# A two-layer decoder trunk on one core: first attention reordered, the expert loop's hidden values in two halves, slot sums made once, heads alternating in stick-breaking

## The reference

```
for i in range(2):
    h = rms_norm(x, attn_norm[i])
    x = x + (swa_sink_attention if i == 0 else stick_breaking_attention)(h, ...)
    h = rms_norm(x, ffn_norm[i])
    x = x + (swiglu if i == 0 else moe_swiglu)(h, ...)
out = rms_norm(x, final_norm)
# swa: q, k, v = split(h @ w_qkv + b_qkv); 16 query heads, 2 key/value heads of 64; window of 128
#      s = q k' / 8 + bias[bucket(distance)]; p = softmax over keys and one learned sink; (p v) @ w_o
# stick-breaking: z = q k' / 8, s < t only; log_fail = log_sigmoid(-z)
#      a = exp(log_sigmoid(z) + reverse cumsum of log_fail, without itself); (a v) @ w_o; 16 heads of 64
# swiglu: (silu(h Wg) * (h Wu)) Wd, width 2816
# moe: each token takes the top 2 of 8 experts by a router; an expert is a swiglu of width 3584
```

## Time and profile before

| | |
|---|---|
| median of 3 runs (lowest, highest) | 1461.12 us (1460.49, 1463.1) |
| the profiled execution, its span | 1462.36 us, 1460.6 us |
| PE busy | 1417.1 us (97%) in 7235 matmul instructions |
| DVE busy, ACT busy, Pool busy | 1089.2 us (75%), 922.3 us (63%), 45.7 us (3%) |
| bytes moved by DMA | 430.99 MB, mean 295 GB/s |

### The profile page before, as it was taken

One profiled execution on the slowest core, in us unless ns is written; L12 is line 12 of the kernel. 1 busy time (PEld: TensorE's weight loads), 2 busy tenths in 40 slices (PEclk: granted clock), 3 DMA queues, 4 the chain that ended last, 5 costly groups with the idle time before them and its releaser, 6 DMA issues.

```text
span 1460.6 us, 19448 instructions
## 1 busy us (share of the span) xinstructions
PE 1417.1 (97%) x7235; PEld 1183.3 (81%) x7235; DVE 1089.2 (75%) x813; ACT 922.3 (63%) x763; POOL 45.7 (3%) x34
## 2 busy tenths in 40 slices
PE   7899999999999999999999999999999999999997
PEld 6778999979876888788788788878878878887885
DVE  5645444464435788888898898888889889888886
ACT  4454434343444677777777777777777777777775
POOL 0110000000000000000000010000000001000000
PEclk9899999999999999999999999999999999999999
DMA  9414554555405799999999999999999999999992
GB/s 340 162 64 159 196 174 144 202 188 174 144 1 202 292 378 369 340 396 379 325 396 387 349 366 391 373 340 396 374 330 395 391 347 364 392 371 337 393 372 112
DMA packets 186320, 430.99 MB, mean 295 GB/s; under 512 B 8170, under 2 KB 13348, under 8 KB 186276
## 3 DMA queue, kind: packets, MB, share of 16 engines
q1 hardware_dynamic: 180628, 416.88, 78.4%
q0 software_dynamic: 2736, 9.96, 2.4%
q10 hardware_dynamic: 2912, 3.53, 0.8%
HBM read 422.99 MB, written 7.36 MB: 295 GB/s over the span
## 4 chain that ended last, share of the span: by engine, by line
PE 89%; DVE 5%; ACT 3%; issue 2%; DMA 0%; POOL 0%; DVEq 0%; ACTq 0%; POOLq 0%
PE bank L1269 87%; DVE low L513 2%; PE bank L1631 2%; ACT high L508 2%; DVE inT_low L1167 1%; DVE h L931 1%; DMA consts<-in_consts 0%; PE bank L1426 0%; PE bank L1308 0%; DVE peak L1015 0%; ACT h L752 0%; ACT h L698 0%; DVE work L1081 0%; DVE x L913 0%; ACT work L808 0%
## 5 line engine op out<-in xcount | busy, mean ns | idle before, releaser
L513 DVE TENSOR_TENSOR low<-raw,high 128x2048 fp32r<-128x2048 f32 x397 | 899.1, 2275 | 244.7 <-ACT high L508 244.2
L508 ACT CAST high<-raw 128x2048 fp32r<-128x2048 f32 x397 | 754.3, 1902 | 326.8 <-PE bank L1269 321.5
L1269 PE MATMUL bank<-high,inT_high 128*128 128x512 f32 (+1 forms) x1016 | 401.7, 395 | 4.0 <-DVE low L513 3.1
L1269 PE MATMUL bank<-high,inT_low 128*128 128x512 f32 (+1 forms) x1016 | 395.2, 389 | 0.0
L1269 PE MATMUL bank<-low,inT_high 128*128 128x512 f32 (+1 forms) x1016 | 394.6, 388 | 0.0
L1269 PEld LDWEIGHTS bank<-high,inT_high 128*128 128x128 f32 x1016 | 191.3, 188 | 46.2 <-issue 6.2
L1269 PEld LDWEIGHTS bank<-high,inT_low 128*128 128x128 f32 x1016 | 191.3, 188 | 40.3
L1269 PEld LDWEIGHTS bank<-low,inT_high 128*128 128x128 f32 x1016 | 191.7, 189 | 37.3
L1269 PE MATMUL bank<-high,hid_high 128*128 128x512 f32 x528 | 208.2, 394 | 8.2 <-DVE hid_low L1174 5.7
L1269 PE MATMUL bank<-high,hid_low 128*128 128x512 f32 x528 | 205.7, 390 | 0.0
L1269 PE MATMUL bank<-low,hid_high 128*128 128x512 f32 x528 | 205.6, 389 | 0.0
(11 more groups left out here) (163 smaller groups left out, 697.1 us busy)
## 6 DMA issues: line engine op xcount, KB each, us to landing
raw<-in_moe_w_gate SPq DMA_DIRECT2D x112, 1024.0 KB, 7.5
raw<-in_moe_w_up SPq DMA_DIRECT2D x112, 1024.0 KB, 7.6
raw<-in_moe_w_down SPq DMA_DIRECT2D x112, 1024.0 KB, 7.3
raw<-in_sb_w_qkv SPq DMA_DIRECT2D x12, 1024.0 KB, 5.0
raw<-in_ffn_w_down SPq DMA_DIRECT2D x11, 1024.0 KB, 4.8
raw<-in_ffn_w_gate SPq DMA_DIRECT2D x10, 1024.0 KB, 5.1
raw<-in_ffn_w_up SPq DMA_DIRECT2D x10, 1024.0 KB, 5.1
raw<-in_swa_w_qkv SPq DMA_DIRECT2D x4, 1024.0 KB, 10.7
```

Of the source, the lines that this page charges most:

```text
L508: nc.scalar.copy(high[n % SPLIT][:, :, 0:c], raw[r][:, :, 0:c]).then_inc(high_done, 1)
L513: nc.vector.tensor_tensor(low[n % SPLIT][:, :, 0:c], raw[n % RAW][:, :, 0:c], high[n % SPLIT][:, :, 0:c].bitcast(F32), ALU.subtract).then_ ...
L1269: return nc.tensor.matmul(out, lhsT, rhs, start=start, stop=stop, **kw)
```

## The change

- Units: keys and values come first (`kv0`, units 0 and 1, as features, values then transposed), the queries after (`q0`, units 2 to 5). The banks of the first attention are given by hand.
- Start: the first norm's gain row is loaded as one row and spread by two matmuls (`gain`); PE starts with matmuls on ones (`warm_up`). The small loads move from Sync's queue to ACT's, the router's to Pool's. DVE copies the bias rows; Pool stores them and reads them back.
- PE waits for `hankel` and makes the toeplitz matmuls right after keys and values, then the queries of groups 0 and 1, scores 0 and 1, the queries of groups 2 and 3, and so on. Scores and values issue the two heads of a pair in turn, in both attentions. The two masks of a stick-breaking head become one matmul of 256 columns.
- Norms 1 to 3: only the first unit after the norm is split ahead of it; the splits of the units behind follow the splits of the input. `keep_clock` has fewer matmuls.
- Expert loop: `hid_high` and `hid_low` are used in halves by turns (`half_of`). The last hidden transpose goes between the two units of down 5; `transposed_rows` goes behind gate 6. ACT makes the gathered high parts before the last hidden cast, with a wait for up 6. The sums "slots" are gone: `next_slots` keeps those of "next", and "first slots" are made once ahead of the loop.

```diff
-    add("qkv0", None, ("q", 1), None, ("q", 3), None, "v")
+    add("kv0", None, ("kv", 0))
+    add("q0", None, ("q", 1), None, ("q", 3))
...
+        def half_of(b):
+            return slice(b % 2 * HALF, (b % 2 + 1) * HALF)
...
-            sp.dma_start(gain_row[:, :], a["attn_norm"][0:1].to_broadcast([P, D])).then_inc(gain_loaded, 16)
...
+            pool.dma_start(router[:, :, :], a["moe_router"][0].rearrange("(t p) e -> p t e", p=P)).then_inc(router_loaded, 16)
+            taken(pool, "bias rows")
+            pool.dma_start(bias_dram.ap(), bias_rows).then_inc(rows_stored, 16)
+            pool.wait_ge(rows_stored, 16)
+            pool.dma_start(hankel.rearrange("p (h k) -> p h k", h=H),
+                           bass.AP(bias_dram, 1, [[1, P], [2 * WINDOW, H], [1, WINDOW]])).then_inc(hankel_loaded, 16)
...
+            act.dma_start(first_gain, a["attn_norm"][0:1]).then_inc(gain_loaded, 16)
...
             split_to(0)
             input_high("hT0")
+            split_to(1)
+            load_gain(1)
             split_to(SPLIT - 1)
...
             for n in range(4):
                 b = full(act, ("toeplitz", n))
                 freed(nc.scalar.copy(flipped[:, n * HALF:(n + 1) * HALF], b), ("toeplitz", n))
+            b = full(act, "v")
+            freed(nc.scalar.copy(v_swa[:, :, :].rearrange("p t s -> p (t s)"), b[:, 0:TB * KV * HD]), "v")
+            split_to(AT["q0"] + SPLIT)
+            nc.scalar.preload_act_table(ACT.Exp)
+            split_to(AT["q0"] + 1 + SPLIT)
+            all_exponentials(0)
+            all_exponentials(1)
+            split_to(AT["q0"] + 2 + SPLIT)
+            act.wait_ge(bias_ready, 4)
+            probs_transposed(0)
+            probs_transposed(1)
+            exponentials(2, range(GROUP // 2), True)
+            input_part_high("oT0", 0)
+            input_part_high("oT0", 1)
...
+            split_to(end("wo0") + 1)
             norm(1, added("wo0"))
+            input_high("hT1")
             split_to(end("wo0") + SPLIT)
-            input_high("hT1")
             load_gain(2)
...
-                split_to(end(("ffn", kind, b)) + SPLIT - 1)
+                split_to(end(("ffn", kind, b)) + (1 if (kind, b) == ("down", FFN_BLOCKS - 1) else SPLIT - 1))
...
                     elif last_hidden:
+                        if not last:
+                            full(act, ("u", BLOCKS - 1), i)
+                            for q in range(2):
+                                gathered_part("gather", q, i)
                         hidden_high(BLOCKS - 1)
                         split_to(n + SPLIT - 1)
-                        if not last:
-                            for q in range(2):
-                                gathered_part("gather", q, i)
-                taken(act, "slots", i)
+                act.wait_ge(slots_ready, i + 1)
...
+            b = full(dve, "bias rows")
+            freed(V.tensor_copy(bias_rows, b[0:H, 0:2 * WINDOW]), "bias rows")
             norm(0)
...
+            split_to(AT["q0"] + SPLIT)
+            queries(0)
+            queries(1)
+            biased(0)
+            shifts(0)
+            split_to(AT["q0"] + 1 + SPLIT)
+            biased(1)
+            shifts(1)
+            inverses(0)
+            inverses(1)
+            queries(2)
+            queries(3)
+            biased(2)
+            shifts(2)
+            biased(3)
+            input_part_low("oT0", 0)
+            input_part_low("oT0", 1)
+            shifts(3)
...
-            norm(3, "wo1", [AT["wo1"] + dh + 1 + SPLIT for dh in range(DH)])
+            norm(3, "wo1", N_MOE)
...
-                            p = full(dve, "slots", i)
-                            steps.mark(V.tensor_copy(slot_sum[:, :], p[:, 0:3]))
+                            steps.mark(V.tensor_copy(slot_sum[:, :], next_slots[:, :]))
...
                         hidden_low(BLOCKS - 1)
+                        if not last:
+                            gathered_part("gather", 0, i * 2 + 3)
                         split_to(n + SPLIT - 1)
                         if not last:
-                            for q in range(2):
-                                gathered_part("gather", q, i * 2 + (q + 3))
+                            gathered_part("gather", 1, i * 2 + 4)
...
+            pe.wait_ge(ones_set, 1)
+            warm_up(1)
...
+            by_features([("kv", 0)], AT["kv0"])
             pe.wait_ge(hankel_loaded, 16)
             for m in range(4):
                 filled(mm(begin(pe, ("toeplitz", m)), flip, hankel[:, m * HALF:(m + 1) * HALF], True, True), ("toeplitz", m))
+            taken(pe, ("kv", 0))
+            b = begin(pe, "v")
+            for tb in range(TB):
+                ins = nc.tensor.transpose(b[:, tb * P:(tb + 1) * P], vT_swa[:, tb * P:(tb + 1) * P], ident)
+            filled(ins, "v")
+            by_features([("q", 0), ("q", 1)], AT["q0"])
...
+            swa_scores(0)
+            swa_scores(1)
+            by_features([("q", 2), ("q", 3)], AT["q0"] + 2)
+            swa_scores(2)
+            swa_transpose(0)
+            swa_scores(3)
+            swa_transpose(1)
             taken(pe, "v")
+            swa_values(0)
+            swa_values(1)
             from_heads(0)
...
+                z = [begin(pe, ("z", n, half)) for half in range(2)]
+                for kb in range(TB):
+                    for half in range(2):
+                        heads = slice(half * HD, (half + 1) * HD)
+                        mm(z[half][:, kb * SEQ:SEQ + kb * P], kT[heads, n, kb * P:(kb + 1) * P],
+                           qT[heads, n, kb * P:SEQ], kb == 0, False, skip_group_check=True)
...
                     used_up(ins, n0 + k)
+                    if b == BLOCKS - 2 and k == 0:
+                        transposed_hidden(BLOCKS - 1, i)
...
                     if kind == "gate" and b >= 1:
                         transposed_hidden(b - 1, i)
-                    elif kind == "up" and b == 0:
-
-                        pe.wait_ge(place_ready, i + 1)
-                        pe.wait_ge(weights_ready, i + 1)
-                        slot_sums("slots", i)
+                        if b == BLOCKS - 1 and not last:
+                            transposed_rows(i)
...
-                    elif kind == "down" and b == BLOCKS - 2:
-                        transposed_hidden(BLOCKS - 1, i)
-                        if not last:
-                            transposed_rows(i)
```

More of the change, by code:

```diff
@@ new lines, in plan, with swa_scores @@
+    u.use("bias rows", 0)
+    for dh in range(DH):
+        u.use(("gain", dh), 1 + dh, counted=False)
+    for j in range(4):
+        u.use(("hT0", j), 3 + j)
+    u.use("biases", 7)
+    u.use(("kv", 0), 0)
+    for n, bank in enumerate((1, 2, 7, 3)):
+        u.use(("toeplitz", n), bank)
+    u.use(("q", 0), 4)
+    u.use(("q", 1), 5)
+    u.use("v", 6)
+    def swa_scores(g, banks):
+        for half in range(2):
+            u.use(("s1", g, half), banks[half])
+        for half in range(2):
+            u.use(("s0", g, half), banks[2 + half])
@@ L235, in plan @@
         u.use(("u", b), 2 + b % 2)
-        if b == 0:
-            u.use("slots", 7)
-        else:
+        if b >= 1:
             u.use(("hidT", b - 1), 6 + (b - 1) % 2)
@@ L1033, in _ @@
[L1033 to L1041 removed]
+                        b = full(dve, (kind, g, half))
```

428 lines of the change are left out of this document (206 added, 222 removed).

## The result

The changed kernel takes 1424.47 us (median of 4 runs, 1423.72 to 1424.95), the kernel before 1460.8 (1460.4 to 1463.1): a ratio of 0.9746, 95% interval 0.9731 to 0.9761. The profiled run took 1424.04 with a span of 1422.2, so 38.4 us are gone from the span. 30.1 were forecast, with a median of 1431.0 in a range of 1420 to 1442.

A forecast was written before the change was run, and what follows sets the result against it. TensorE, busy 97% of the span, was taken as the bound. Gains of 16.1 + 2.4 (loop), 3.0 (attention), 2.2 + 1.6 + 0.3 (norms) and 4.5 (stick-breaking) made 30.1 us: median 1431.0, range 1420 to 1442.

The forecast's parts named there:

- rival (1): First attention: the band read lands early, by 24; 9 us more gain, 1422; chance 0.17.
- the attention term: First attention: 3 us of an ideal 21.5 left; refuted by a PE pause before toeplitz under 5 or over 20 us.
- seam terms: End of an expert-loop item: late matmuls and their restarts vanish, 0.76 + 0.48 + 0.62 + 0.20 us an item.
- term of 0.46 for the slot sums: Expert loop: removing the slot sums saves PE 0.36 plus a restart of 0.10 us an item.
- beside a DVE that waits each unit: Expert loop: one small DVE copy more replaces the slot sums, on a DVE taken to have waits in each unit.
- remainders: Expert loop: 0.2 us an item taken off, as for a later scatter whose landing DVE awaits.
- I take 0: the transfer of the same pieces is the nearest row: First attention: band read from Pool's queue taken no later than ACT's 19.4 us, landing at 33.4; possible delay 0 to 38.
- a first product at 15.4: Norm 0, kernel start: first product near 15.4 instead of 16.89, a gain of 1.5 us.
- Steps of 4.2: Stick-breaking head loop: 4.2 us a step with hand-overs, against PE's 5.04 before; six full steps save 0.8 each.
- The chain that was to set the step: Stick-breaking: values, scores, clamp, two ACT passes, maximum and sums add to 7.9 us per two steps, 3.95 a step.
- The 2.6 taken off for more half clock: Stick-breaking: 2.6 us deducted because PE then pauses in each step, leaving a gain of 4.5.
- Rivals (2) to (5): (2) longer attention, 1439, 0.13; (3) no stick-breaking gain, 1435.5, 0.10; (4) late subtracts, 1440 or 1449.5, 0.08; (5) slow band read, 1469, 0.04.

The follow-up runs named there:

- e2: Changed kernel with the order at an item's end undone (hidden and row transposes behind the last but one down block): 1441.28 us, ratio 0.9865.
- e1: Changed kernel with the slot sums back as four matmul instructions in every item: 1424.74 us, ratio 0.9750.
- e6: Changed kernel with VectorE's chain of slots cut in two, the second half moved to the item's second block: 1420.21 us, ratio 0.9736.
- e5: Changed kernel with the band read issued from ScalarE's queue again instead of GpSimd's: 1432.62 us, ratio 0.9824.
- e8: Changed kernel with the probabilities of the first attention's third softmax group made by VectorE instead of GpSimd: 1418.63 us, ratio 0.9725.
- e4: Changed kernel with the weight split moved back ahead of the input parts at the second and third norm alone: 1434.29 us, ratio 0.9816.
- e7: Changed kernel with VectorE's low parts of the second attention's output written one stick-breaking step later: 1419.51 us, ratio 0.9731.
- e3: Changed kernel with stick-breaking scores, masks (128 columns) and values head by head again: 1432.53 us, ratio 0.9807.
- e10: Changed kernel with slot chain cut, low parts later, third probabilities on VectorE, and the first query unit ahead of the band's flips: 1407.79 us, ratio 0.9640.
- e0: Changed kernel run once more, unchanged: 1422.92 us, ratio 0.9746.

## Why the prediction came out as it did

It was 1431.0 with a range of 1420 to 1442; 1424.47 is 6.5 below the forecast, inside the range, just outside the forecast's own 1425 to 1437, and nearest to rival (1) at 1422. One of its own signs also speaks against a part of it: PE's pause before toeplitz was 4.35 us, and under 5 was to refute the attention term.

**The loop, 18.5 against 18.2: right in sum, with one wrong term.** The seam terms 0.76 + 0.48 + 0.62 + 0.20 (2.06) measured 2.19 in e2. The term of 0.46 for the slot sums measured nothing in e1. The step that failed is "beside a DVE that waits each unit": at that place DVE ran from 705 to 714 us with no wait, and its chain became the wait; e6, which cuts the chain, gets 0.65 an item. That the sum is right all the same is luck: 0.13 too little for the seam and the 0.2 taken off for "remainders" nearly make up for the 0.46. The last item gave 3.0 for 2.4.

**First attention, 7.3 against 3.0: the band read was mis-sized.** "I take 0: the transfer of the same pieces is the nearest row" is the step that failed: the nearest row was of another queue. 11.2 us measured, 19.4 taken, and e5 shows that this is worth 8 us (8.1 in the median, 7.7 in the stretch). The price of the other queue had been bounded on one side only, 0 to 38 us later; the early landing stood as rival (1) with 0.17, but without this mechanism. The queries started 10 us earlier than forecast (31.1 for 41.1), yet the projection only 4.4: 5.6 were given back downstream, among them a wait of 4.3 for GpSimd where 3 were foreseen, and 2.8 lost at half clock behind it and 1.6 behind the pause for the third scores, instead of 1.5 in all; e8 gets 5.7 back. The rest was not split up. A part of the 7.3 is the start of the kernel, next.

**The start.** 1.5 us were forecast from a first product at 15.4 instead of 16.89. The changed kernel's was at 15.54 (1.35 of the 7.3), but over the changed kernel and the twelve of the experiments it lies between 14.69 and 16.66. With one trace of before this term can be called neither right nor wrong.

**Norms.** 2.2 and 2.1 against 2.2 and 1.6; e4 gives 2.05 a subtract. Norm 3 gained 0.8, and the router lost 0.85: before the first expert product the changed kernel has the slot sums of the first item, with a wait of its own, where none stood. I had costed that part at nothing. It was read, not tested.

**Stick-breaking, 8.4 against 4.5: the clock had the wrong sign, and two errors cancel.** The first two scores gained 2.5 (2.3 forecast). The loop gained 4.5, near the 4.8 before the deduction, but not in the way that was told. "Steps of 4.2" were 3.9 where nothing else stood in DVE's queue, and 5.9 and 7.4 where the low part did; that wait was in no part of the sum, and e7 shows it to be 5.0 us with its clock. The chain that was to set the step is also added up wrongly: its terms make 7.4, not 7.9, so 3.7 a step, under PE's own 3.9. The 2.6 taken off for more half clock failed: one stretch stood in the loop as before, and the one in the values' projection (3.4 us from 369 on) went away, 1.4 gained. That 1.4 isn't owed to the order of the heads: e3 has the old order and 21.8 us there too. What took it away is open.

Rivals (2) to (5) are out: attention didn't lengthen, stick-breaking gained, the seam's subtracts were in time, and GpSimd wrote the pieces faster, not slower.

## What to carry to other kernels

After taking an instruction off the bounding engine, look in the queues of the others for what stood under it: here a chain of nine small VectorE operations, hidden until then, took back the whole gain of the removed matmuls, and moving half of it one block on freed 0.65 us an item. A conversion that waits for another engine belongs behind the work that the bounding engine waits for, not ahead of it; this was the case in stick-breaking and at the norms, and by e10's rows with the queries' copies, where it wasn't tried. And a transfer moved to another queue has another price: bound it on both sides, and look at packets, not only at bytes.

## What the runs showed of the hardware

- A 1 MB read in 512-byte pieces beside a full weight queue: 18.7 to 19.4 us from ScalarE's queue, 11.2 from GpSimd's. By e5's packet counts against the changed kernel's that is 509 bytes a packet on the one and 3.9 KB on the other.
- GpSimd and VectorE slow one another where VectorE reads two operands of which none lies in a PSUM bank: 2.89 to 4.83 us on GpSimd, 0.16 to 1.85 on a tiny VectorE operation, and, beside GpSimd's selects, 2.29 to 2.72 for VectorE's subtracts (three in 8.15 us) and 1.08 to 3.14 for one of the selects.
- A pause costs more than itself where the granted clock then falls from 1.00 to 0.50, that is from 2.4 to 1.2 GHz: 4.3 us of waiting in the changed kernel became 1.3 in e8, and the gain was 5.7. Whether such a stretch comes can differ between executions of the same instructions: behind the dense block e1, e2, e3 and e7 have one and e0 and e6 have none, with the same program up to there. What decides it no run here shows.
